# A macaron decoder step on one core: the last and first four units of a stage, taken by halves of the tokens

## What is computed

```
f1 = swiglu(rmsnorm(x, g0), ...);        x = x + 0.5 * rmsnorm(f1, g1)
y  = token_mixing(rmsnorm(x, g2), ...);  x = x + rmsnorm(y, g3)
f2 = swiglu(rmsnorm(x, g4), ...);        x = x + 0.5 * rmsnorm(f2, g5)
swiglu(h) = (silu(h @ w_gate) * (h @ w_up)) @ w_down        # 1024 -> 2816 -> 1024
rmsnorm(v, g) = v / sqrt(mean(v^2) + 1e-6) * g              # mean over the 1024 features of a token
```

## Time and profile before

| | us |
|---|---|
| median of 3 runs | 1213.54 (1212.35 to 1218.38) |
| the profiled execution | 1212.42 |
| its span, first to last instruction | 1210.6 |
| PE busy | 1146.4 (95% of the span) |
| DVE busy | 612.5 (51%) |
| ACT busy | 327.6 (27%) |
| POOL busy | 43.3 (4%) |
| mean granted TensorE clock | 0.968 of full |

### The profile page before, as it was taken

One profiled execution on the slowest core, in us unless ns is written; L12 is line 12 of the kernel. 1 busy time (PEld: TensorE's weight loads), 2 busy tenths in 40 slices (PEclk: granted clock), 3 DMA queues, 4 the chain that ended last, 5 costly groups with the idle time before them and its releaser, 6 DMA issues.

```text
span 1210.6 us, 21567 instructions
## 1 busy us (share of the span) xinstructions
PE 1146.4 (95%) x8994; PEld 1124.2 (93%) x8994; DVE 612.5 (51%) x959; ACT 327.6 (27%) x449; POOL 43.3 (4%) x57
## 2 busy tenths in 40 slices
PE   6999999999999898999898989899999999999994
PEld 6999999999999897998777889899999999999994
DVE  5533343333445755889767517664343433343344
ACT  5311222112222323421234343332122221122120
POOL 0000000000000000210221100000000000000002
PEclk9999999999999979999899989899999999999997
DMA  6313232223222211332500001303232322232211
GB/s 228 104 53 104 88 103 70 87 87 105 69 104 70 70 49 53 76 90 83 31 19 19 1 1 55 105 4 126 67 117 70 102 73 87 87 101 72 87 53 74
DMA packets 34235, 92.17 MB, mean 76 GB/s; under 512 B 10240, under 2 KB 10752, under 8 KB 34048
## 3 DMA queue, kind: packets, MB, share of 16 engines
q1 hardware_dynamic: 32592, 87.67, 24.0%
q10 hardware_dynamic: 1584, 3.68, 0.8%
HBM read 88.05 MB, written 3.28 MB: 75 GB/s over the span
## 4 chain that ended last, share of the span: by engine, by line
PE 83%; DVE 11%; issue 3%; ACT 3%; ACTq 0%; DVEq 0%
PE ps L305 24%; PE ps L307 24%; PE ps L306 24%; DVE a L429 2%; PE ps L947 1%; PE ps L330 1%; DVE mixf L800 1%; ACT wh L284 1%; DVE wl L289 1%; PE ps L953 1%; PE ps L954 1%; PE ps L343 1%; ACT sq L411 1%; PE ps L1389 1%; DVE xx L1126 0%
## 5 line engine op out<-in xcount | busy, mean ns | idle before, releaser
L305 PE MATMUL ps<-xh,wh 128*128 128x272 f32 x1840 | 540.1, 294 | 24.2 <-DVE xl L471 15.8
L307 PE MATMUL ps<-xh,wl 128*128 128x272 f32 x1840 | 536.2, 291 | 0.0
L306 PE MATMUL ps<-xl,wh 128*128 128x272 f32 x1840 | 533.7, 290 | 0.0
L305 PEld LDWEIGHTS ps<-xh,wh 128*128 128x128 f32 x1840 | 350.5, 190 | 26.6 <-DVE wl L289 15.5
L306 PEld LDWEIGHTS ps<-xl,wh 128*128 128x128 f32 x1840 | 351.1, 191 | 0.1
L307 PEld LDWEIGHTS ps<-xh,wl 128*128 128x128 f32 x1840 | 350.2, 190 | 0.0
L284 ACT ACTIVATE wh<-raw 128x1024 fp32r<-128x1024 f32 (+1 forms) x163 | 167.9, 1033 | 306.6 <-PE ps L307 202.4
L289 DVE TENSOR_TENSOR wl<-raw,wh 128x1024 fp32r<-128x1024 f32 (+1 forms) x163 | 192.7, 1203 | 57.0 <-ACT wh L284 56.6
L307 PE MATMUL ps<-hh,wl 128*128 128x272 f32 x704 | 202.8, 288 | 0.0
L305 PE MATMUL ps<-hh,wh 128*128 128x272 f32 x704 | 202.6, 288 | 0.0
L306 PE MATMUL ps<-hl,wh 128*128 128x272 f32 x704 | 202.1, 287 | 0.0
(11 more groups left out here) (294 smaller groups left out, 827.0 us busy)
## 6 DMA issues: line engine op xcount, KB each, us to landing
raw<-in_w_gu SPq DMA_DIRECT2D x88, 512.0 KB, 3.6
raw<-in_w_d SPq DMA_DIRECT2D x32, 512.0 KB, 3.5
raw<-in_w_in SPq DMA_DIRECT2D x19, 512.0 KB, 3.5
raw<-in_w_d SPq DMA_DIRECT2D x16, 384.0 KB, 3.1
raw<-in_w_out SPq DMA_DIRECT2D x8, 512.0 KB, 3.5
x<-in_x ACTq DMA_DIRECT2D x8, 272.0 KB, 6.5
out_y<-x SPq DMA_DIRECT2D x8, 272.0 KB, 2.1
con<-in_con ACTq DMA_DIRECT2D x1, 1158.5 KB, 9.3
```

Source lines behind the costliest of these rows:

```text
L305: pe.matmul(out[:, n], wh[:, s, j], right_h[:, j, col], start=opens and j == order[0], stop=False)
L306: pe.matmul(out[:, n], wh[:, s, j], right_l[:, j, col], start=False, stop=False)
L307: last = pe.matmul(out[:, n], wl[:, s, j], right_h[:, j, col], start=False, stop=closes and j == order[-1])
```

## The change

At each of the three ends of a stage the work is cut by halves of the tokens.

- `last_units_pe`: units 0 to 3 of the last eight are done whole, as before. Then units 4 to 7 are done for half 0 of the tokens, one after the other (24 matmuls each), and after that for half 1. Between the matmuls of half 1 stand the small matmuls of half 0's norms (sums and spreads of 3 matmuls for a half where there were 6).
- Each half has its own statistics: the functions `half_...`, `var_dve` and `square_dve` are those of before on 272 tokens and 3 columns. For rows 4 to 7 leaving PSUM, squares, cross product and addition go by halves; rows 0 to 3 go whole.
- `hand_over_act` and `hand_over_dve` write out the order of ACT and DVE from there to the last row of x: half 0's rows stand among half 1's statistics and the splits of the next stage's four tiles, then half 1's rows. An update, an addition, xh and xl of a half row are one instruction each (`update_dve`, `add_dve`, `high_act`, `low_dve`).
- `ramp_pe`: the first four units of the next stage for half 0, row by row, with half 1's small matmuls in between, then for half 1; rows 6 and 7 of half 1 again unit by unit.
- In the FFNs the down products of rows 0 to 3 of the last group are taken out of PSUM at slightly other places, and a square root of a constant stands early in the last group on ACT.
- At the end (`final_dve`, `final_pool`) half 0's rows are made and stored by DVE and SP during half 1's products; half 1's rows are then shared with POOL as before; there are 16 stores of a half row instead of 8.
- The unit number that is skipped lies between w_in and w_out (`OUT0 = NIN + 1`) instead of behind w_out; w_out's tiles move one slot on. The transfer of the states in the mixer (L762) waits for n_sum 5 instead of 3.

The diff, cut (8 columns of indentation are taken off; `leave_half` for the mixer copies instead of adding):

```diff
-SKIP = FFN2 - 1
+SKIP = MIX0 + NIN
...
-def product(pe, out, s, order, right_h, right_l, before=None, opens=True, closes=True):
+def product(pe, out, s, order, right_h, right_l, before=None, opens=True, closes=True, parts=(0, 1)):
...
-        for n in range(2):
+        for n in parts:
...
+def half_squares_dve(dve, n, h, d):
...
+    dve.wait_ge(S("h_sq0"), here)
+    dve.tensor_tensor(a3[:, 0, c], a3[:, 0, c], more[:, 0, c], ADD).then_inc(S("n_ssq"), 1)
+    dve.wait_ge(S("h_sq"), here)
+    dve.wait_ge(S("h_x"), here)
+    dve.tensor_tensor(a3[:, 1:3, c], a3[:, 1:3, c], more[:, 1:3, c], ADD).then_inc(S("n_ssq"), 1)
...
+def rows_dve(dve, n, h, first, last):
+    for k in range(first, last):
+        update_dve(dve, n, h, k)
         if k:
+            low_dve(dve, n, h, k - 1)
+        add_dve(dve, n, h, k)
+    if last == KD:
+        low_dve(dve, n, h, KD - 1)
...
+def last_units_pe(pe, n, u0, first, order, right_h, right_l, free):
+    for d in range(4, KD):
+        split_ready(pe, u0, 0, first + d)
+        free(d)
+        product(pe, pair(d - 4), d - 4, order, right_h, right_l, parts=(0,)).then_inc(S("half_done"), 1)
+    def second(d, lo, hi):
+        return product(pe, pair(d - 4), d - 4, order[lo:hi], right_h, right_l, opens=lo == 0, closes=hi == KD, parts=(1,))
+    second(4, 0, 5)
+    half_sums_pe(pe, n, 0, 0)
+    second(4, 5, 8).then_inc(S("unit_done"), 1)
+    if n < 5:
+        half_sums_pe(pe, n, 0, 1)
+    second(5, 0, 2)
+    half_spread_pe(pe, n, 0, 0)
+    second(5, 2, 8).then_inc(S("unit_done"), 1)
+    second(6, 0, 8).then_inc(S("unit_done"), 1)
+    if n < 5:
+        half_spread_pe(pe, n, 0, 1)
+    second(7, 0, 8).then_inc(S("unit_done"), 1)
+def ramp_pe(pe, n, u):
+    def come(h, j):
+        pe.wait_ge(S("n_xl"), row(n, h, j) + 1)
+    pe.wait_ge(S("n_rb"), mark(n, 0, 1) + 1)
+    for j in range(KD):
+        come(0, j)
         for s in range(3):
-            product(pe, pair(s), s, (j,), xh, xl, opens=j == 0, closes=False)
-        if j == 1:
-            spread_root_pe(pe, n)
+            if j == 0:
+                split_ready(pe, u, 0, s)
+            product(pe, pair(s), s, (j,), xh, xl, opens=j == 0, closes=j == KD - 1, parts=(0,))
+        if j == 2:
+            half_sums_pe(pe, n, 1, 0)
+        if j == 3:
+            half_sums_pe(pe, n, 1, 1)
+            half_spread_pe(pe, n, 1, 0)
         if j == 4:
             split_ready(pe, u, 0, 3)
-            pe.wait_ge(S("n_rb"), n + 1)
-            product(pe, pair(3), 3, range(5), xh, xl, closes=False)
+            product(pe, pair(3), 3, range(5), xh, xl, closes=False, parts=(0,))
         if j > 4:
-            product(pe, pair(3), 3, (j,), xh, xl, opens=False, closes=False)
+            product(pe, pair(3), 3, (j,), xh, xl, opens=False, closes=j == KD - 1, parts=(0,))
+        if j == 5:
+            half_spread_pe(pe, n, 1, 1)
+    pe.wait_ge(S("n_rb"), mark(n, 1, 1) + 1)
+    for j in range(KD - 2):
+        come(1, j)
+        for s in range(4):
+            product(pe, pair(s), s, (j,), xh, xl, opens=j == 0, closes=False, parts=(1,))
     for s in range(4):
-        product(pe, pair(s), s, (KD - 2, KD - 1), xh, xl, None if s else input_ready, opens=False).then_inc(S("unit_done"), 1)
+        product(pe, pair(s), s, (KD - 2, KD - 1), xh, xl, None if s else lambda j: come(1, j), opens=False, parts=(1,)
+                ).then_inc(S("unit_done"), 1)
+def hand_over_act(act, n, u):
+    for d in range(4, KD):
+        half_squares_act(act, n, 0, d)
+    half_root_act(act, n, 0, 0)
+    split_hi(act, u, 0, 0, KD)
+    half_squares_act(act, n, 1, 4)
+    half_rb_act(act, n, 0, 0)
+    high_act(act, n, 0, 0)
+    split_hi(act, u, 0, 1, KD)
+    half_root_act(act, n, 0, 1)
+    high_act(act, n, 0, 1)
+    half_squares_act(act, n, 1, 5)
+    split_hi(act, u, 0, 2, KD)
+    half_rb_act(act, n, 0, 1)
+    high_act(act, n, 0, 2)
+    half_squares_act(act, n, 1, 6)
+    high_act(act, n, 0, 3)
+    split_hi(act, u, 0, 3, KD)
+    half_squares_act(act, n, 1, 7)
+    half_root_act(act, n, 1, 0)
+    high_act(act, n, 0, 4)
+    high_act(act, n, 0, 5)
+    half_rb_act(act, n, 1, 0)
+    high_act(act, n, 0, 6)
+    half_root_act(act, n, 1, 1)
+    high_act(act, n, 0, 7)
+    high_act(act, n, 1, 0)
+    half_rb_act(act, n, 1, 1)
+    for k in range(1, KD):
+        high_act(act, n, 1, k)
+def hand_over_dve(dve, n, u, leave_half):
+    for d in range(4, KD):
+        leave_half(0, d)
+        half_cross_dve(dve, n, 0, d)
+        half_squares_dve(dve, n, 0, d)
+    var_dve(dve, n, 0)
+    half_rec_dve(dve, n, 0, 0)
+    leave_half(1, 4)
+    half_cross_dve(dve, n, 1, 4)
+    split_lo(dve, u, 0, 0, KD)
+    half_squares_dve(dve, n, 1, 4)
+    rows_dve(dve, n, 0, 0, 1)
+    square_dve(dve, n, 0)
+    rows_dve(dve, n, 0, 1, 2)
+    leave_half(1, 5)
+    half_cross_dve(dve, n, 1, 5)
+    half_rec_dve(dve, n, 0, 1)
+    split_lo(dve, u, 0, 1, KD)
+    rows_dve(dve, n, 0, 2, 3)
+    half_squares_dve(dve, n, 1, 5)
+    split_lo(dve, u, 0, 2, KD)
+    leave_half(1, 6)
+    half_cross_dve(dve, n, 1, 6)
+    rows_dve(dve, n, 0, 3, 4)
+    leave_half(1, 7)
+    half_cross_dve(dve, n, 1, 7)
+    half_squares_dve(dve, n, 1, 6)
+    half_squares_dve(dve, n, 1, 7)
+    var_dve(dve, n, 1)
+    rows_dve(dve, n, 0, 4, 5)
+    half_rec_dve(dve, n, 1, 0)
+    split_lo(dve, u, 0, 3, KD)
+    rows_dve(dve, n, 0, 5, 6)
+    square_dve(dve, n, 1)
+    rows_dve(dve, n, 0, 6, 7)
+    half_rec_dve(dve, n, 1, 1)
+    rows_dve(dve, n, 0, 7, 8)
+    rows_dve(dve, n, 1, 0, 8)
...
+def final_dve(dve, leave_half):
...
+    for d in range(4, KD):
+        leave_half(0, d)
+        half_squares_dve(dve, 5, 0, d)
+    var_dve(dve, 5, 0)
+    half_rec_dve(dve, 5, 0, 0)
+    leave_half(1, 4)
+    some(0, 1)
+    half_squares_dve(dve, 5, 1, 4)
+    some(1, 3)
+    leave_half(1, 5)
+    some(3, 4)
+    half_squares_dve(dve, 5, 1, 5)
+    some(4, 6)
+    leave_half(1, 6)
+    some(6, 7)
+    half_squares_dve(dve, 5, 1, 6)
+    some(7, 8)
+    leave_half(1, 7)
+    half_squares_dve(dve, 5, 1, 7)
+    var_dve(dve, 5, 1)
+    half_rec_dve(dve, 5, 1, 0)
...
 def ffn_pe(pe, q, u0, n):
...
+            last_units_pe(pe, 4 * q + 1, u, 0, range(nf), hh, hl, down_free)
...
 def ffn_act(act, q, u0, n):
...
             if s == 1:
                 silu_act(act, q, 0, f0, nf - 1)
+                if g == 2:
+                    act.activation(st2[:, 1, 6:7], ones[:, 0:1], ACT.Sqrt)
...
 def ffn_dve(dve, q, u0, n):
...
+    def leave_half(h, d):
+        if h:
+            unit_done(dve, u - KD, 0, d)
+        else:
+            dve.wait_ge(S("half_done"), 4 * (n // 2) + d - 3)
+        dve.wait_ge(S(f"d_out{q}"), 4 + KD + d + 1)
+        c = part_of(h)
+        dve.tensor_tensor(f[:, d, c], ps[:, 2 * (d - 4) + h, 0:H], f[:, d, c], ADD).then_inc(S("f_half"), 1)
+    if n == 5:
+        final_dve(dve, leave_half)
+    else:
+        hand_over_dve(dve, n, u, leave_half)
...
-OUT0 = NIN
+OUT0 = NIN + 1
...
 def mixer_pe(pe):
...
         product(pe, pair(m), (OUT0 + m) % 4, late, xh, xl, y_ready, opens=False).then_inc(S("unit_done"), 1)
-    for m in range(2, KD):
+    for m in range(2, 4):
         split_ready(pe, MIX0, 0, OUT0 + m)
-        pe.wait_ge(S("o_out"), m - 1)
-        product(pe, pair(m % 2), (OUT0 + m) % 4, Y_ORDER, xh, xl
-                ).then_inc(S("unit_done"), 2 if m == KD - 1 else 1)
+        product(pe, pair(m), (OUT0 + m) % 4, Y_ORDER, xh, xl).then_inc(S("unit_done"), 1)
+    def out_free(m):
+        pe.wait_ge(S("o_out"), m - 3)
+    last_units_pe(pe, 3, MIX0, OUT0, Y_ORDER, xh, xl, out_free)
...
 def _(sp):
...
+        sp.wait_ge(S("y_first"), k + 1)
+        sp.dma_start(o["y"][:, k, part_of(0)], x[:, k, part_of(0)]).then_inc(S("out"), 16)
+    for k in range(KD):
+        if k in BY_POOL:
+            sp.wait_ge(S("y_pool"), BY_POOL.index(k) + 1)
         else:
-            sp.wait_ge(S("x_ready"), 2 * KD + sum(not by_dve(5, j) for j in range(k + 1)))
-        sp.dma_start(o["y"][:, k], x[:, k]).then_inc(S("out"), 16)
-    sp.wait_ge(S("out"), (6 + KD) * 16)
```

More of the change, by code:

```diff
@@ L321, in window, with sums_pe, spread_root_pe @@
             return slice(n * H + (0, P, H - P)[j], n * H + (0, P, H - P)[j] + P)
[L323 to L330, removed]
-            m.then_inc(S("n_sum"), 1)
[L333 to L339, removed]
+        def sums_pe(pe):
+            pe.wait_ge(S("n_ssq"), 1)
+            for t in range(6):
+                m = pe.matmul(ps[:, 6, t:t + 1], a3[:, 0, window(t)], ones[:, 0:1], start=True, stop=True)
+            m.then_inc(S("n_sum"), 1)
+        def spread_root_pe(pe):
+            pe.wait_ge(S("n_rec"), 1)
             for t in range(6):
@@ new lines, in part_of, with trio, mark, half_sums_pe @@
+        def part_of(h):
+            return slice(H * h, H * h + H)
+        def trio(h):
+            return slice(3 * h, 3 * h + 3)
+        def mark(n, h, second=0):
+            return 1 + 4 * (n // 2) + (2 * h + second if n < 5 else h)
```

(37 more changed lines are left out.)

431 lines of the change are left out of this document (209 added, 222 removed).

## The result

In interleaved runs the changed kernel took 1210.09 us (median of 12, 1201.85 to 1212.86), the kernel before 1215.36 (12, 1212.35 to 1220.44): a ratio of 0.9945, 95% interval 0.993 to 0.996. On a second chip it was 0.9962 (0.9945 to 0.9979); one execution of the change there took 1593.02 us at a mean granted clock of 0.649 and is left out, and the median of the other 11 is 1212.39. So the change is faster by 0.4 to 0.6%, some 4 to 7 us, where 1200.5 was forecast; the time lies above the range, which ended at 1209. The profiled execution took 1210.43 us, with a span of 1208.6.

What follows compares the result with a forecast made beforehand. TensorE bounds FFN1; at the three boundaries a chain through VectorE does. 1212.4 - 7.7 - 4.0 - 5.6 + 4.5 = 1199.6 us for the profiled execution; the runs' median is 1.1 above: 1200.7, said as 1200.5, range 1194 to 1209.

Steps and rivals of the forecast that it cites:

- Where TensorE waits: Both boundaries: waits for half 0's statistics (1.7, 2.75), half 1's sum (1.1, 1.15), row 3 (1.2, 0.8), fifth unit (6.05, 2.5).
- The two for half 1's sum: TensorE's waits for half 1's sum of squares: 1.1 us at the first boundary, 1.15 at the second.
- VectorE's prices: Instructions of 272 elements: 0.436 us, about 0.50 with gain, with 0.08 overlap between two that follow each other.
- the slower rival: VectorE sets the pace at the boundaries, half-size instructions costing 12% or more above the line; 7 in 100 for slower.
- The end: From FFN2's last products to the last store: last rows done at 1202.4, store's tail 2.6, 5.6 us less.
- the term of the clock: After the remaining waits TensorE's clock runs low: three stretches of 1.5 us cost each, 4.5 us more.
- its upper bound of 12: The clock term's upper bound: eight low stretches, 12 us; the lower bound was none.
- 17.3: Gains before the clock term: 7.7 at the first boundary, 4.0 at the second, 5.6 at the end.
- the 7.7 and 4.0: Forecast gains: first boundary from 73.3 to 65.6 us, 7.7 less; second from 66.7 to 62.7, 4.0 less.
- The rival "the clock": Every wait, also the short ones, brings a low stretch: eight, 12 us instead of 4.5, so 1208; 8 in 100.
- discount: In the clock term: half of each low stretch falls in time VectorE sets anyway, a reason for taking only three.

Runs made afterwards that it cites:

- the dummies: Changed kernel with 240-column matmuls whose result nobody reads filling TensorE's waits, 80 and 58 in the two boundaries: 1198.46 us, ratio 0.9844 to the kernel before.
- the kernel with the ramp filled: Changed kernel with unread 240-column matmuls only around half 1's first sums (6 before, 8 behind): 1203.79 us, ratio 0.9889 to the kernel before.
- 80 and 37 in the two boundaries and 23 at the end: Kernel before the change with unread 240-column matmuls in its own waits, 13 of them ahead of the ramp: 1205.17 us, ratio 0.9901 to the kernel before.
- 36 in place of 13: Kernel before the change with its waits filled by unread matmuls, 36 of them ahead of the ramp: 1214.65 us, ratio 0.9971 to the kernel before.
- the early split: Changed kernel with the tile of the mixer's fifth unit split before the first units' tanh, shift and leave work: 1207.07 us, ratio 0.9921 to the kernel before.

## Why the prediction was wrong

**Where TensorE waits: right.** Of the waits laid out by hand those of 1.7, 1.2, 6.05, 2.75, 0.8 and 2.5 us came as 1.81, 1.07, 6.18, 2.66, 0.63 and 2.63. The two for half 1's sum were overestimated (1.1 and 1.15 against 0.30 and 0.38). **VectorE's prices: right**, to 0.01 us, and with them the verdict on the slower rival. **The end: right.** 5.6 forecast, 4.9 seen, in spite of 1.5 lost to the low stretch behind the fifth unit at 818.2, which belongs to the clock's term.

**The step that failed is the term of the clock**, "I take three, 4.5 us more". The profile has seven low stretches at the places that the change touches, not three, and they are 3.4 to 10.2 us long, not the 3.3 of the one row of before from which the price was taken. What the changed waits and prices would have given stood in the sum as 17.3; the boundaries at full clock are 66.2 and 62.8 against 65.6 and 62.7. The difference to the change's profile is 6.9 (73.1 less 66.2) and 7.3 (70.1 less 62.8), and 1.5 behind FFN2's fifth unit: 15.7 us, three and a half times the term and over its upper bound of 12. 1195.1 without the term plus 15.7 is 1210.8; the execution took 1210.43. That it comes out within 0.4 is luck in part, since the boundaries were off by 0.6 and 0.1 and the end by 0.8 the other way. The stated 1200.5 also began from a median of three, 1213.54; over 12 executions the kernel before has 1215.36, so that the gain in it, 13.0 us, is to be read against the 5.3 measured.

Three mistakes are in that one number. The **length** was taken from the shortest stretch of the old trace, while the same old trace had 17.1 us in the first boundary and 13.7 in the second, as its PEclk of 0.82 and 0.84 over 49.2 and 42.6 us says. At 0.45 us a us these are worth up to 7.7 and 6.2 us, no less than the 7.7 and 4.0 that the boundaries were to gain: the sum set old boundaries at a low clock against new ones at the full clock, and 4.5 us was all that it gave back. The **place**: I counted a stretch for a long wait, but the longest begin behind waits of 0.30 and 1.07 us, and of 0.38 and 0.63, with six small matmuls between them (427.09 to 428.99, low from 429.1). The rival "the clock" had the right mechanism ("every wait, also the short ones") and a chance of 8 in 100, and its eight stretches were still priced at 1.5. The old trace had such a place, inside the mixer, which no row of the prediction shows: a wait of 1.29 us, twenty one-column matmuls, and from 698.8 on 10.3 us at the low clock with TensorE at work throughout.

```profile
697.13 2.86 PE L1239 MATMUL ps<-con,mixf 128*128 128x1 f32 x20 [1.29 <-ACT mixf L1282]
698.80:709.10 10.30, 10.30 (x49) 0.50 0.00 0
```

The Trainium skill ("TensorE: Matmul & The Clock Gate", section on psum-queue depth-cycling) tells of short idles between groups of matmuls that made the clock swing; the prediction held against it that no row showed one below 1.7 us that did, and the new trace agrees with the skill, by the 0.30 and 1.07 us. The **discount**, "half of each stretch falls in time that VectorE sets anyway", does not come out of the runs. In the changed kernel the dummies took 20.7 and 17.0 us of low clock away for 6.9 and 7.3 us, 0.33 and 0.43 us a us, against the 0.45 of a stretch with products in it throughout; 3.7 of the 20.7 us lay inside the wait for the fifth unit and need not have cost anything. Nor does it describe the old kernel: there 10.7 and 6.8 us less of it gave 3.8 and 3.1, which is 0.36 and 0.45. So halves and dummies are in part the same gain: the old boundaries lost time to the low clock, and either can take it back.

**How much of the spread is the clock.** Each timed execution comes with its span and mean granted clock, and (1 - clock) x 2 x span is its time at the lower level. In the 12 runs of the change this goes with the span at 0.45 us per us (0.29 to 0.49 in the other kernels); with 0.45 of it taken off, the 12 spans have a standard deviation of 1.2 us where they had 3.1. The mixer between its fifth unit and its last four, where the two kernels' code is the same, took 284.7 us in the profile of the change and 292.7 in that of the kernel with the ramp filled (window of each):

```profile
463.50:748.20 284.70, 264.97 (x2105) 0.95 0.21 45
```
```profile
459.60:752.30 292.70, 270.91 (x2106) 0.92 0.19 44
```

Low stretches there sum to 30 and 48 us, and the 18 more at 0.45 are the 8 us. The ramp's profiled execution was thus the slowest of its six, and says nothing against its median.

## What to carry to other kernels

When work is moved so that a tensor engine has products to do in a stretch where it waited, price that stretch at the clock it will be granted, not at full speed: read how long the low stretches of the old trace are, not only that there are some, and compare old and new at the same clock. Where short waits and bursts of small matmuls stay, try dummies first: here 80 and 37 in the two boundaries and 23 at the end brought the old kernel more (12 us) than the change did (4 to 7), and 80 and 58 brought the changed kernel 14 on top of that; count them so that they end before the data comes, for 36 in place of 13 gave back most of it. And a wait behind a chain may be an order: the early split took 5.5 us of wait away by moving two calls, 1.4 of which stood again 8 us later.

## What the runs showed of the hardware

That the granted clock can fall behind waits as short as 0.30 and 1.07 us, or 0.38 and 0.63, with six small matmuls (one column each) between them, and stay low for 10.2 us while TensorE is busy throughout (10.20 us busy of 10.20 in the windows above). That with 14 matmuls of 240 columns around them it stayed at 1.00 in all six ramps profiled, where it was low in 8 of 10 without. And that low stretches differ between executions of the same code, by 18 us in one stretch of 290, at a cost of about 0.45 us each; what starts or spares one in a given execution is not settled here.
